# A wait on TensorE's own count in front of every slot of an expert gather

## The reference, cut to what matters

```
def peer_ffn(h, wq, subkeys, u, v):
    ...
    def expert_block(args):
        hc, ec, gc = args
        uc = jnp.take(u, ec, axis=0)
        a = jnp.einsum('cd,ced->ce', hc, uc)
        act = jax.nn.gelu(a, approximate=False) * gc
        vc = jnp.take(v, ec, axis=0)
        return jnp.einsum('ce,ced->cd', act, vc)
```

## Time and profile before

| what | value |
|---|---|
| median of three executions | 2671.0 us (2654.5 to 2672.6) |
| the profiled execution, own time | 2678.2 us |
| its span in the profile | 2676.4 us |
| stretch that holds all slots | 182 to 1833 us of the span |
| PE busy in the whole span | 2144.8 us (80%) |
| mean granted TensorE clock | 0.908 of 2.4 GHz |

### The profile page before, as it was taken

The page is one execution under the profiler, slowest core; times in us unless marked ns, Lnnn a source line. Parts: engine busy times, 40 slices in busy tenths (PEclk is TensorE's granted clock), DMA queues, the critical chain, the costliest instruction groups (busy, mean ns, idle before and its releaser), DMA issues. The chain is left out here.

```text
span 2676.4 us, 27484 instructions
## 1 busy us (share of the span) xinstructions
PE 2144.8 (80%) x8468; PEld 1131.5 (42%) x8468; DVE 1352.2 (51%) x2888; ACT 776.8 (29%) x2244; POOL 1047.9 (39%) x1107
## 2 busy tenths in 40 slices
PE   4888778667777787888777758777979998988997
PEld 2455534222333343354433323324645544655553
DVE  5765567766456567474675655343431222342222
ACT  2243223232333334343333334232411002221101
POOL 4035555667666556655566566561000000000000
PEclk9898888888998998999988879998879999988999
DMA  9748888999999999999999999895239997208996
GB/s 371 291 188 301 312 307 322 392 373 396 406 413 412 404 392 362 398 354 374 349 341 367 391 368 370 328 366 206 79 130 404 418 418 282 86 0 358 417 417 282
DMA packets 236992, 879.66 MB, mean 329 GB/s; under 512 B 23282, under 2 KB 29954, under 8 KB 214338
## 3 DMA queue, kind: packets, MB, share of 16 engines
q0 software_dynamic: 149488, 543.97, 53.2%
q1 hardware_dynamic: 87380, 334.23, 31.6%
HBM read 877.07 MB, written 1.05 MB: 328 GB/s over the span
## 5 line engine op out<-in xcount | busy, mean ns | idle before, releaser
L2195 DVE CUSTOM_DVE_ANT_0 arena<-arena,PS 128x1024 f32<-128x1024 f32 x512 | 625.1, 1221 | 523.4 <-DMA arena<-in_peer_u_dram,IDX 401.5
L915 POOL DMA_INDIRECT arena<-in_peer_v_dram,IDX x512 | 502.7, 982 | 465.7 <-PE PS L1515 261.3
L1515 PE MATMUL PS<-arena 128*128 128x512 f32 x1024 | 519.7, 651 | 183.8 <-issue 95.3
L1515 PE MATMUL PS<-arena,JK 128*128 128x512 f32 x1024 | 515.5, 646 | 165.8 <-ACT JK L1071 94.6
L912 POOL DMA_INDIRECT arena<-in_peer_u_dram,IDX x512 | 500.3, 977 | 314.0 <-issue 146.8
L1515 PEld LDWEIGHTS PS<-arena 128*128 128x128 f32 x1024 | 201.5, 207 | 472.4 <-issue 435.9
L1515 PEld LDWEIGHTS PS<-arena,JK 128*128 128x128 f32 x1024 | 200.2, 205 | 455.3 <-issue 420.9
L1058 ACT ACTIVATE ACTV<-DOT 128x1 f32<-128x1 f32 x512 | 101.8, 199 | 761.2 <-DVE DOT L2195 461.3
L1908 PE MATMUL PS<-arena,HT 128*64 128x256 f32 x2048 | 238.0, 385 | 18.9 <-DMA arena<-in_w_down_dram 12.3
L1908 PEld LDWEIGHTS PS<-arena,HT 128*64 128x64 f32 x2048 | 149.4, 138 | 98.4 <-DMA arena<-in_w_down_dram 21.6
L1066 ACT ACTIVATE GACT<-ACTV,GATE 128x1 f32<-128x1 f32 x512 | 150.8, 295 | 27.9 <-issue 5.1
(11 more groups left out here) (351 smaller groups left out, 1945.3 us busy)
## 6 DMA issues: line engine op xcount, KB each, us to landing
arena<-in_w_gate_dram SPq DMA_DIRECT2D x64, 1024.0 KB, 16.5
arena<-in_w_up_dram SPq DMA_DIRECT2D x64, 1024.0 KB, 18.6
arena<-in_w_down_dram SPq DMA_DIRECT2D x64, 1024.0 KB, 15.3
arena<-in_w_ada_dram SPq DMA_DIRECT2D x22, 2048.0 KB, 12.4
arena<-in_w_in_dram SPq DMA_DIRECT2D x11, 2048.0 KB, 16.8
arena<-in_peer_wq_dram SPq DMA_DIRECT2D x10, 2048.0 KB, 9.5
arena<-in_w_out_dram SPq DMA_DIRECT2D x6, 2048.0 KB, 11.0
arena<-in_peer_u_dram,IDX POOLq DMA_INDIRECT x512
```

Of the source, the lines that this page charges most:

```text
L915: pool.indirect_dma_start(out=GV[b], out_offset=None, in_=v_rows, in_offset=off).then_inc(v_loaded[b], 16)
L1515: last = pe.matmul(PO[:, half, :], DIAG[n % DIAGS], GV[BUF[n]][:, half * 512:(half + 1) * 512], start=(j == 0), stop=False, skip_group_che ...
L2195: dve.tensor_tensor_reduce(GU[BUF[n]], GU[BUF[n]], HP[tt].rearrange("p b n -> p (b n)"), 1.0, 0.0, ALU.mult, ALU.add, DOT[:, s:s + 1]).the ...
```

## The change

In front of the matmuls of every slot but the first, TensorE waits until its own count expert_added has reached n, that is until the matmuls of slot n-1 have been written and counted. Nothing else is changed: no instruction is moved, and no other engine's program differs.

```
                 pe.wait_ge(v_loaded[BUF[n]], 16 * LOADS[n])
                 pe.wait_ge(diag_ready, n + 1)
+                if n:
+                    pe.wait_ge(expert_added, n)
                 for half in range(2):
                     last = pe.matmul(PO[:, half, :], DIAG[n % DIAGS], GV[BUF[n]][:, half * 512:(half + 1) * 512],
                                      start=(j == 0), stop=False, skip_group_check=True)
```

## The result

The median rose from 2662.7 us (4 runs, 2642.7 to 2672.6) to **2708.6 us** (4 runs, 2695.6 to 2709.9): the ratio is 1.0166, with a 95% interval of 1.0107 to 1.0224. The change costs 46 us. The forecast was 2676 us, in a range of 2652 to 2702.

A forecast was written before the change was run, and what follows sets the result against it. It took a ring of 8 buffer pairs, with gathers, DMA and POOL's queue nearly full and PE third, as the bound. A median of 2671 us plus 0 for fast and 5 for slow slots gave 2676 us, range 2652 to 2702.

The forecast's parts named there:

- I therefore set the fast slots to 0: Back-to-back slots at the high clock: 0.44 us lost on each, up to 342 slots, adds 0 at the kernel's end.
- the term for the signal: Between a slot's last matmul and the next slot: PE's wait for its own count takes 0.20 us, 0.30 at most.
- The comparison of paces: Within a burst: a slot with the wait takes 2.16 us, still under the 2.50 us of POOL's two gathers.
- Its place ... leftover from the burst before: At a burst's first slot: only earlier leftover work, 7 us, could move POOL's wait, and PE's 9.60 us idle covers it.
- The +5 us for slow slots: Slots at 1.2 GHz: 47 in bursts lose 0.53 us each, 25 us, of which 20% meets a waiting POOL.
- The rival of the clock: Bursts starting at 1.2 GHz: breaks between slots keep the clock low for one slot more; 2706 us, chance 0.10.
- the marks that the prediction set: In the slots' stretch: clock step wrong if granted clock falls under 0.87 or mean slot matmul rises over 690 ns.
- PE as the bound: Over the slots: every slot's loss on PE reaches the end, 150 us, giving 2821 us; chance 0.04, at least in part.
- the gain: At bursts' first slots: shorter idle stretches keep the clock up, saving 42 us, giving 2629 us; chance 0.06.
- The fourth rival: At slot starts: PE in effect waits already, so the change does nothing; 2671 us, chance 0.03.
- The pauses of 0.15 us: Sign of being right: before slots in a burst, PE idles 0.15 to 0.30 us for its own matmuls, some 300 times.
- not 100: Sign on the slots' stretch: longer by over 100 us would mean that PE is the bound.
- the mark of 20: Sign on POOL's wait on PE, near 261 us: growth by more than 20 us makes the POOL step wrong.

The follow-up runs named there:

- the second chip: Follow-up comparison of the changed kernel and variants on another chip, where the kernel before ran at 2547.9 us and the changed one had ratio 0.9998.
- plain1: The kernel before, unchanged, profiled on the same chip as the follow-up runs beside it; 2670.5 us.
- lag4: The changed kernel with the wait set three slots back (slot n waits for count n-3), against the kernel before; 2671.9 us, ratio 1.0004.
- lag2_b: The changed kernel with the wait one slot further back (count n-1), against the kernel before on a chip with late counts; 2661.8 us, ratio 0.9999.
- longer_b: The kernel before with a third matmul of 256 columns in each slot and no wait, against the kernel before; 2683.4 us, ratio 1.0061.
- firsthalf: The changed kernel, waiting on PE's own separate semaphore raised by the previous slot's first matmul, against the kernel before; 2681.2 us, ratio 1.0050.
- again_b: The changed kernel run once more on a chip with late counts, against the kernel before; 2715.0 us, ratio 1.0171.
- again_c: The changed kernel run once more on a further chip with late counts, against the kernel before; 2723.7 us, ratio 1.0209.
- longown: The changed kernel with a third matmul of 256 columns in each slot, against the kernel before; 2734.8 us, ratio 1.0267.
- again: The changed kernel run once more on a chip without late counts, against the kernel before; 2548.2 us, ratio 0.9998.
- lag2: The changed kernel with the wait one slot further back (count n-1), against the kernel before on a chip without late counts; 2548.3 us, ratio 0.9996.

## Why the prediction was wrong

**The step that failed is "I therefore set the fast slots to 0", and under it the term for the signal.** The prediction priced the wait for the own count from one normal place, 0.30 us after line 1394, and one for ScalarE's diagonal, 0.15 us, and held it for the same in every slot. On the second chip it is (0.15 us, and no cost), and there the 0 for the fast slots holds. On the others some 35 to 40 waits in the 512 take 2 to 7 us, which the prediction had no term for. In the first comparison PE loses 115 us to small waits (295 slots at 0.39 us, where the prediction had up to 342 at 0.44 and so 150 us), and 156 us (179 - 23) more to pauses; the term that was set to 0 measured about 46 us at the end of the kernel.

**The comparison of paces was right as far as it went.** 2.16 us a slot were forecast and 2.10 measured, against POOL's 2.50. But 2.10 us is the pace between pauses. The mean with the pauses in it can be taken from the traces, over the slots that follow a slot directly on PE and whose diagonal was ready when that slot's matmuls ended. It stands in the second column, in us from start to start. The third has POOL's waits, beyond 0.30 us each, for adds that had just ended (us in all), the fourth the time by which the adds end behind their diagonals:

| kernel, comparison | mean pace | POOL's waits | add behind diagonal | ratio |
|---|---|---|---|---|
| before, first | 2.00 | 201 | 4.9 | |
| plain1, third | 1.99 | 206 | 5.1 | |
| lag4, third | 2.06 | 205 | 5.5 | 1.000 |
| lag2_b, fourth | 2.41 | 191 | 6.6 | 1.000 |
| longer_b, fourth | 2.31 | 213 | 6.6 | 1.006 |
| firsthalf, fourth | 2.57 | 218 | 7.6 | 1.005 |
| changed, first | 2.71 | 232 | 9.1 | 1.017 |
| again_b, third | 2.74 | 244 | 9.2 | 1.017 |
| again_c, fifth | 2.81 | 246 | 9.3 | 1.021 |
| longown, fifth | 2.89 | 251 | 11.0 | 1.027 |

With the pauses in it the changed kernel's pace isn't under POOL's 2.50 us any more, while that of `lag2_b`, with pauses and no small waits, is. On the second chip `again`, with small waits and no late counts, has 2.22 us and 1.000. So each term alone cost little or nothing, 0 to 0.5% for the pauses (`lag2_b`, `firsthalf`) and 0 for the small waits, and both together 1.7 to 2.1%. That the pace is the reason is the best reading that the runs allow: it goes along with the cost in ten traces, but the small waits alone were measured only on the chip without late counts, and no run varied the pace of POOL.

**"Its place ... leftover from the burst before" was the right place to look.** The prediction named what could move POOL's waits, work left over from the burst before, and sized it at 7 us from the 0.44 us alone. A single pause took up to 7 us.

**The end of the range.** The +5 us for slow slots can't be told apart from nothing. The rival of the clock fell: mean clock of the stretch 0.92 after 0.90, mean matmul 660 and 657 ns after 646 and 651, neither past the marks that the prediction set. Most long pauses do bring the clock down for a slot (29 of the 38 over 2 us, starts of tiles included, are followed by a slot of over 2.9 us), but the slots over 2.9 us are 49 in the changed kernel as they were 50 before; `again_b` has 59 and `plain1` 56. PE as the bound with 150 us reaching the end did not come either: PE lost 270 us and 46 came through. Nor did the gain. The fourth rival, no change at all, has the number of the second chip, but not its reason: 291 slots paid the 0.39 us there.

**The marks.** The pauses of 0.15 us came as named, about 300 of them; the stretch grew by 20 us, not 100. POOL's wait on PE rose by 16 us (261.3 to 277.5), under the mark of 20, and 11 more went to "remote". Taken together that is 27 us, and the mark should have been set on POOL's whole idle time in front of line 915: +29 us.

**What could have been seen.** The trace of before held it, in lines that the prediction did not read. POOL's waits in front of line 915 (us, times), and one of them:

```profile
  PE PS L1515: 261.3, 108
  issue: 133.2, 374
  remote: 70.2, 29
...
1621.89 0.93 POOL L915 DMA_INDIRECT arena<-in_peer_v_dram,IDX  x1 [2.83 <-PE PS L1515]
```

This gather is for slot 443 and needs the adds of slot 435, the last of the four in the first line of the earlier trace rows, which end at 1606.76 + 7.03 = 1613.79. POOL stood from 1619.06 to 1621.89 for something done 5 us before it came. Of the 465.7 us, 109 are of this kind, in 48 stalls; the 2.81 us of the earlier trace rows are not, there the add had just ended. Had I asked of each such wait which add it needed and when that ended, a second wait on the same semaphore, in the busiest engine, would have had another price than 0.20 us.

The Trainium skill ("Perfetto Trace Analysis", Tensor Engine Instruction) says that a matmul's semaphore is raised when PSUM has acknowledged the data, travels then, and that the end shown in a profile is modelled. It names no duration for the last part. Here it was 0.15 us from the modelled end to the next start in the back-to-back slots on one chip, and on others up to 7.2 us in the changed kernel and 9.2 in `firsthalf`.

## What stays open

Why counts of PE come late on some chips and not on others. Four of the five comparisons had them and one did not. The four after the first ran on four different chips; which one the first ran on isn't known. The trace can't tell a late write into PSUM from a late message about it. That the clock falls in the pauses speaks for an array that has nothing to do; that is an argument and not a measurement. Counts of DVE and ScalarE showed no such lateness in the same traces (in the middle of a tile only 6 of before's slots start over 0.5 us late behind a finished diagonal, none over 1.4 us, and ScalarE starts over 0.5 us late behind a finished dot 3 times in 512), but no kernel was made to look for it. Instruction fetches aren't the cause: of the changed kernel's 38 pauses over 2 us only 2 overlap with one. What the small waits cost by themselves on a chip with late counts was not measured. No version faster than both was found: `lag2` and `lag4` are at 1.000 and do what the kernel without the wait does.

## What to carry to other kernels

A wait for a count that PE raises itself is not a constant: most often it was 0.15 us here, and in four comparisons of five 35 to 40 of the 511 waits took 2 to 7 us, in one kernel up to 9. Where such a wait is needed, set it a few slots back: `lag4` was at 1.000 on the chip where the strict one was at 1.017, and `lag2` at 1.000 on another with late counts. Before pricing a new wait on a semaphore, look how those who wait for it now fare: check for each of their long waits when the work behind the count had ended. And compare paces with the pauses in them, since two losses that each fit into an engine's room may not fit together.

## What the runs showed of the hardware

- Between chips the same kernel differed by 4.5 to 4.9% (2547.9 us against 2662.7 to 2671.5). POOL's waits for counts of adds long finished make up a difference of about 100 us (12 us against 110 to 115). The granted clock over the span was 0.948 in `again` and 0.916 in `again_b`.
- A count of PE arrived up to 7.2 us after the modelled end when PE itself waited for it in the changed kernel, 9.2 us in `firsthalf`, and POOL got one 14 us after (1745.40 to 1759.74) when PE ran on. At 33 of the changed kernel's 35 pauses over 2 us in the middle of a tile POOL, waiting for the same count, started 0.122 to 0.125 us after PE, so the lateness is in the count and not in one waiting engine.
- In the changed kernel the slots behind pauses of 4.5 to 7.5 us took 3.4 to 3.75 us in place of 1.95 (a slot at the low level of the clock, 1.2 GHz, takes 3.75); the mean clock of the stretch did not fall (0.92 after 0.90).
- The second matmul of each slot left out made the kernel 0.6% faster on one chip and 0.4% slower on another. PE's busy time fell by 252 and 286 us, and the mean granted clock of the span by 0.1 (0.929 to 0.820, and 0.907 to 0.809).
